# Even mixing part, sample group: an unread 128-column product of the identity among the narrow state products

## The chip, the cores and the metric

One core of a Trainium2 chip runs the whole kernel. The metric is the device time of one execution in microseconds; each version is executed several times and the median counts.

## What is computed

Two layers of a recurrent decoder are applied to a prompt of 2048 tokens and to a sample group of 8 sequences of 8 tokens each. The even layer runs retention heads and RWKV-7 heads side by side, the odd layer a gated delta rule. The sample sequences start from stored states, so each product of a query or a key with a state uses another state per sequence:

```python
# retention, per sequence b: queries times the state it starts from
o = jnp.einsum('bhck,bhkv->bhcv', qc * q_scale, S) + intra
# RWKV-7, per sequence b: keys and receptances read the state
s_kk = jnp.einsum('bhvk,bhk->bhv', S, kk_t)
S = S * exp(lw_t) - s_kk[..., None] * (kk_t * a_t)[:, :, None, :] + v_t[..., None] * k_t[:, :, None, :]
y = jnp.einsum('bhvk,bhk->bhv', S, r_t)
```

For the prompt one state serves all 128 tokens of a tile; for the samples each of the 8 states serves 8 tokens.

## The kernel before

The kernel runs four phases with a barrier after each: the even projection, the even mixing part (`mix_even_phase`), the odd projection, the odd mixing part. Tokens are worked in 17 tiles of 128: 16 of the prompt and, as tile number `PT`, the 64 sample tokens. The even mixing part is a software pipeline written out by hand. In a step, `t` is the tile whose right side, solve and outputs are made, `n` the tile ahead of it (scores, retention), `m` and `q` those ahead of that, and `p` the tile before, whose output projection (`project`, eight parts of six 512-column products) is laid between the others. Each engine has its own queue, in the order of the code, and they wait for each other by semaphores; what TensorE does is therefore exactly the order of the calls in the loop at the end of its block.

Two places of TensorE's queue handle the sample states:

- `ret_out(n)` with `n == PT` (line 1777 on): after the waits for the attention scores and for the loaded retention states it makes 32 products, each with a 64x128 stationary block (`sre`, a view of `me_xs`) and 8 moving columns of `qsT`, into banks `A_` and `B_`. VectorE copies them to `QST` (line 1350), and then the outputs of retention are made with the identity as moving operand, followed by `turn_mix(PT - 1)`, eight transposes.
- `sample_state_products(t)` with `t == PT` (line 1581 on), called first in `right_side(PT)`: 64 products, each with a 64x64 stationary block of `srw` (views of `me_th`, `me_kkr`, `me_ex2`) and 16 moving columns of `KR`, into bank `BX`; then `sample_ret_state(0, 0)`, VectorE's copy to `KST` (line 1344, in the trace `me_IL`), and `sample_ret_state(0, 1)`.

After these come, for tile `PT`, the products of `right_side` and `outputs_of_values` (a 128-column product of `KST` and the identity and two 64-column ones, eight times), `solve`, `project(PT - 1, 0)` and `outputs_of_solved`. All operands are plain f32 except those of `project`, which are rounded; a plain f32 product is two instructions (passes) in the trace, each with its own weight load. So the 32 products of the first place are 64 passes and the 64 of the second are 128 passes. A product's line in the trace is that of the helper `mm`, L1567; a transpose's is L1570.

Bank `BY` takes the results of `level_T`, which ScalarE copies out and counts in `s_ptc`; for tile `PT` there are two such levels (2 and 4). Later, `sample_ret_state` overwrites `BY`.

Of the kernel before, what the change touches and what calls it, by code (L numbers as in the profile page):

```python
# [12 lines left out]
P = 128  # L13
D = 1024
KD = D // P
SEQ, DEC_B, DEC_T = 2048, 8, 8
NS = DEC_B * DEC_T
PT = SEQ // P
# [562 lines left out]
def mix_even_phase(nc, t_in, out):  # L581
# [6 lines left out]
    with ctx:  # L588
# [3 lines left out]
        def sem(n):  # L592
            return new_semaphore(nc, sems, f"me_{n}")
# [16 lines left out]
        ident = ident_sb[:]  # L610
# [82 lines left out]
        A_, B_, C_, D_, BX, BY, BC = bk[3], bk[4], bk[2], bk[6], bk[7], bk[1], (bk[0], bk[5])  # L693
# [37 lines left out]
        s_ptc = sem("T_written")  # L731
# [19 lines left out]
        def levels_of(n):  # L751

            return [b for b in LEVELS[1:] if b < (DEC_T if n == PT else P)]

        LV = [sum(len(levels_of(i)) for i in range(n)) for n in range(NT + 1)]
# [6 lines left out]
        def await_(eng, name, n):  # L762


            if n >= 0:
                eng.wait_ge(E[name], n + 1)
# [798 lines left out]
        def _(pe):  # L1565
            def mm(o, l, r, start=True, stop=True):
                return nc.tensor.matmul(o, l, r, start=start, stop=stop)  # L1567

            def turn(o, i):
                return nc.tensor.transpose(o, i, ident)  # L1570

            def from_state(t, bank, b, which):


                o = bank[:, b * P:(b + 1) * P]
                if t == PT:
                    mm(o, KST[:, b, which, :], ident, start=b == 0, stop=False)
                else:
                    mm(o, KR[t % 2][:, b, which, :], s_wk[:, b].rearrange("p h v -> p (h v)"), start=b == 0, stop=False)

            def sample_state_products(t):
                pe.wait_ge(s_smp, 16 * 4)
                for b in range(4):
                    for q in range(DEC_B):
                        for p0 in (0, 64):
                            o = BX[p0:p0 + 64, b * P:(b + 1) * P].rearrange("p (w c) -> p w c", w=2)
                            last_op = mm(o[:, :, q * 8:q * 8 + 8], srw[b][p0:p0 + 64, q, :], KR[t % 2][p0:p0 + 64, b, :, q * 8:q * 8 + 8])
                last_op.then_inc(s_ks, 1)
                sample_ret_state(0, 0)
                pe.wait_ge(s_ksc, 1)  # L1590
                sample_ret_state(0, 1)

            def right_side(t):
                if t == PT:
                    sample_state_products(t)
                await_(pe, "o_copied", t)
                await_(pe, "state_new", t - 1)
                await_(pe, "mga_read", t)
                await_(pe, "mgb_read", t)
                for b in range(4):  # L1600
                    from_state(t, A_, b, 0)
                    for h in (2 * b, 2 * b + 1):
                        last_op = mm(A_[:, h * WN:(h + 1) * WN], MG[:, h, 0, :], tokV[t % 2][:, h, :], start=False, stop=h == H - 1)
                last_op.then_inc(E["rhs_ready"], 1)

            def outputs_of_values(t):
                await_(pe, "mixT_written0", t - 1)
                for b in range(4):
                    from_state(t, C_, b, 1)
                    for h in (2 * b, 2 * b + 1):  # L1610
                        mm(C_[:, h * WN:(h + 1) * WN], MG[:, h, 1, :], tokV[t % 2][:, h, :], start=False, stop=False)
# [162 lines left out]
            def ret_out(n):  # L1774
                v = tv[n % 2]
                pe.wait_ge(s_tv[n % 2], 16 * (n // 2 + 1))
                await_(pe, "att_written", n)
                await_(pe, "lengths_ready", min(n + 1, PT))
                await_(pe, "q_scaled", n)
                await_(pe, "ret_state_new", n - 1)  # L1780
                if n == PT:
                    for j in range(2):
                        pe.wait_ge(s_smr[j], 16)
                    for b in range(2):
                        for q in range(DEC_B):
                            for k, bank in enumerate((A_, B_)):
                                p0 = 64 * k
                                last_op = mm(bank[:, b * NS + q * 8:b * NS + q * 8 + 8], sre[b][p0:p0 + 64, q, :],
                                             qsT[p0:p0 + 64, b, q * 8:q * 8 + 8])
                    last_op.then_inc(s_qs, 1)  # L1790
                    pe.wait_ge(s_qsc, 1)
                for b in range(2):
                    if n < PT:
                        mm(A_[:, b * 256:(b + 1) * 256], qsT[:, b, :], s_ret[:, b].rearrange("p h v -> p (h v)"), stop=False)
                    for h in (2 * b, 2 * b + 1):
                        o = A_[:, h * RDV:(h + 1) * RDV]
                        if n == PT:
                            mm(o, QST[:, h, :], ident, stop=False)
                        last_op = mm(o, att[:, h, :], v[:, h * RDV:(h + 1) * RDV], start=False, stop=n == PT or h % 2 == 1)
                last_op.then_inc(E["ret_ready"], 1)  # L1800
# [55 lines left out]
            def sample_ret_state(b, r):  # L1856


                at = slice(r * Q, (r + 1) * Q)
                pe.wait_ge(s_mr, 2 * b + 2)  # L1860
                if b:
                    pe.wait_ge(s_mcr, 2)
                for half in range(2):
                    h, p0 = 2 * b + half, 64 * half
                    mm((BY, BX)[r][p0:p0 + 64, :], ks[at, h, :], vmr[h][at].rearrange("p q v -> p (q v)")).then_inc(s_mur, 1)
# [21 lines left out]
            for p, t, n, m, q in STEPS:  # L1887
# [74 lines left out]
                if n is not None:  # L1962
                    level_T(n, 64)
                    ret_out(n)
# [1219 lines left out]
```

## Time and profile before

| what | us |
|---|---|
| median of three executions (lowest, highest) | 3169.6 (3165.99, 3186.61) |
| the profiled execution | 3168.01 |
| its span, first to last instruction | 3166.2 |
| TensorE products, busy | 2978.1 (94% of the span) |
| VectorE, busy | 1864.6 (59%) |
| ScalarE, busy | 1032.0 (33%) |
| mean granted TensorE clock | 0.960 of full |

The busy shares are of the whole span; the granted clock is the share of 2.4 GHz that TensorE received, so that 1.00 is 2.4 GHz and 0.50 is 1.2 GHz. The profiled execution lies 1.6 us below the median. The even mixing part ends at about 1592 us of the span.

### The profile page before, as it was taken

The numbers are of one execution on the slowest core, as the hardware profiler recorded it, in microseconds if no ns is written. First come the engines' busy times: TensorE is split into PE (matmuls) and PEld (weight loads), VectorE is DVE, ScalarE is ACT, GpSimd is POOL, SyncE is SP. The second block draws the span as 40 slices with busy tenths as digits, with TensorE's granted clock in tenths as the row PEclk, the third lists the DMA queues.
The fourth block names the chain that finished last, engine by engine and source line by source line (L and its number), as shares of the span: only waits on it lengthen the run. The fifth ranks groups of instructions, "written<-read, shape, count | busy, mean of one in ns | idle before, by whom it ended". The sixth has DMA issues, their size and how long they took to land. (4 is left out here: it accounts for less than half of the span.)

```text
span 3166.2 us, 88698 instructions
## 1 busy us (share of the span) xinstructions
PE 2978.1 (94%) x38430; PEld 2714.3 (86%) x38430; DVE 1864.6 (59%) x3858; ACT 1032.0 (33%) x2337; POOL 502.9 (16%) x519
## 2 busy tenths in 40 slices
PE   8999999994899999999969999999995899999998
PEld 8999999993788888888769999999995788888886
DVE  4311222324677777777535156777665778887876
ACT  4211111113333443343157122222223344444441
POOL 0000000001333433333300000000001111111112
PEclk9999999996799999999889999999997899999998
DMA  5321212115233333343353221222114223333333
GB/s 166 99 73 60 73 64 69 67 49 170 71 97 115 120 111 118 112 126 122 100 176 110 75 69 61 74 75 70 66 47 158 72 82 96 95 96 95 94 98 127
DMA packets 222915, 302.15 MB, mean 95 GB/s; under 512 B 32184, under 2 KB 163520, under 8 KB 222528
## 3 DMA queue, kind: packets, MB, share of 16 engines
q1 hardware_dynamic: 213376, 266.54, 26.1%
q0 software_dynamic: 9152, 29.94, 3.0%
q8 instruction: 305, 5.00, 0.6%
q14 instruction: 82, 0.67, 0.1%
HBM read 200.70 MB, written 95.71 MB: 94 GB/s over the span
## 5 line engine op out<-in xcount | busy, mean ns | idle before, releaser
L363 DVE SCALAR_TENSOR_TENSOR po_stage<-po_work,po_cw,po_stage 128x424 f32<-128x424 f32 (+1 forms) x360 | 232.1, 645 | 27.6 <-issue 0.9
L476 PE MATMUL po_ps<-po_xnT_hi,po_w_hi 128*128 128x424 f32 x960 | 205.0, 355 | 0.0
L476 PE MATMUL po_ps<-po_xnT_hi,po_w_lo 128*128 128x424 f32 x960 | 204.4, 355 | 0.0
L476 PE MATMUL po_ps<-po_xnT_lo,po_w_hi 128*128 128x424 f32 x960 | 204.1, 354 | 0.0
L270 ACT ACTIVATE po_work<-po_ps 128x424 f32<-128x424 f32 (+1 forms) x120 | 61.6, 514 | 408.3 <-PE po_ps L476 408.3
L476 PEld LDWEIGHTS po_ps<-po_xnT_hi,po_w_hi 128*128 128x128 f32 x960 | 180.2, 188 | 5.2
L476 PEld LDWEIGHTS po_ps<-po_xnT_hi,po_w_lo 128*128 128x128 f32 x960 | 180.4, 188 | 4.5
L476 PEld LDWEIGHTS po_ps<-po_xnT_lo,po_w_hi 128*128 128x128 f32 x960 | 180.2, 188 | 4.6
L476 PE MATMUL pe_ps<-pe_w_hi,pe_xnT_hi 128*128 128x256 f32 x1088 | 154.9, 285 | 4.3 <-DVE pe_w_lo L382 3.6
L476 PE MATMUL pe_ps<-pe_w_lo,pe_xnT_hi 128*128 128x256 f32 x1088 | 153.4, 284 | 0.0
L476 PE MATMUL pe_ps<-pe_w_hi,pe_xnT_lo 128*128 128x256 f32 x1088 | 152.7, 283 | 0.0
L405 DVE TENSOR_SCALAR pe_stage<-pe_work,pe_cw 128x424 f32<-128x424 f32 (+1 forms) x65 | 28.2, 434 | 208.9 <-ACT pe_work L270 157.8
L476 PEld LDWEIGHTS pe_ps<-pe_w_hi,pe_xnT_hi 128*128 128x128 f32 x1088 | 140.8, 193 | 4.8 <-DVE pe_w_lo L382 4.0
L476 PEld LDWEIGHTS pe_ps<-pe_w_lo,pe_xnT_hi 128*128 128x128 f32 x1088 | 141.1, 193 | 0.0
L476 PEld LDWEIGHTS pe_ps<-pe_w_hi,pe_xnT_lo 128*128 128x128 f32 x1088 | 140.5, 192 | 0.0
L195 POOL DMA_DIRECT2D po_raw<-in_w_in_o x60 | 40.4, 677 | 622.4 <-DVE po_w_lo L382 621.8
L405 DVE TENSOR_SCALAR po_stage<-po_work,po_cw 128x424 f32<-128x424 f32 (+1 forms) x120 | 51.9, 433 | 143.8 <-ACT po_work L270 97.2
L195 POOL DMA_DIRECT2D pe_raw<-in_w_in_e x56 | 31.2, 557 | 581.1 <-DVE pe_w_lo L382 578.9
L1567 PE MATMUL me_b<-me_w_hi,me_mixT 128*128 128x512 f32 x272 | 120.8, 444 | 2.6 <-DMA me_ring<-scratch_w_lo 1.7
L270 ACT ACTIVATE pe_stage<-pe_ps 128x256 f32<-128x256 f32 x102 | 39.2, 384 | 254.5 <-PE pe_ps L476 254.4
L2823 PE MATMUL mo_b<-mo_w_hi,mo_mixT 128*128 128x512 f32 x272 | 120.1, 441 | 1.7 <-DVE mo_mixT_lo L2494 1.3
L363 DVE SCALAR_TENSOR_TENSOR pe_stage<-pe_stage,pe_ps 128x256 f32<-128x256 f32 x68 | 28.6, 421 | 157.4 <-ACT pe_stage L270 157.4
(453 smaller groups left out, 7169.3 us busy)
## 6 DMA issues: line engine op xcount, KB each, us to landing
me_ring<-scratch_w_lo SPq DMA_DIRECT2D x68, 512.0 KB, 3.8
mo_c<-scratch_ch_o SPq DMA_DIRECT2D x51, 512.0 KB, 3.5
scratch_ch_o<-po_stage SPq DMA_DIRECT2D x96, 212.0 KB, 1.9
scratch_tok_e<-pe_stage SPq DMA_DIRECT2D x136, 128.0 KB, 1.9
pe_raw<-in_w_in_e POOLq DMA_DIRECT2D x52, 256.0 KB, 3.7
me_xs<-scratch_ch_e SPq DMA_DIRECT2D x17, 768.0 KB, 6.2
po_raw<-in_w_in_o POOLq DMA_DIRECT2D x48, 256.0 KB, 3.8
scratch_ch_e<-pe_stage SPq DMA_DIRECT2D x52, 212.0 KB, 1.9
```

Source lines behind the costliest of these rows:

```text
L195: eng.dma_start(raw[r % RAW][:, :, 0:n], w_in[:, at:at + HK * n].rearrange("p (k n) -> p k n", k=HK)).then_inc(loaded(r)[0], 16)
L270: return nc.scalar.activation(o, i, f, **kw)
L363: return nc.vector.scalar_tensor_tensor(out=o, in0=a, scalar=s, in1=b, op0=op0, op1=op1)
L405: last = nc.vector.tensor_scalar(o, src, k, None, ALU.mult, ALU.bypass)
L476: last = nc.tensor.matmul(out, left.bitcast(F32R), right.bitcast(F32R), start=(i == 0 and k == 0), stop=(i == 2 and k == KD - 1))
L1567: return nc.tensor.matmul(o, l, r, start=start, stop=stop)
L2823: return nc.tensor.matmul(o, l, r, start=start, stop=stop)
```

## The change

A helper `keep_awake` issues a product of the identity with itself, 128 stationary columns and 128 moving ones, into the first 128 columns of `BY`, which nobody reads. In `sample_state_products` one is issued after every four narrow products (eight passes), but not after the last four: 15 in all. In `ret_out(PT)` one is issued in the middle of every four narrow products, 8 in all. There TensorE also waits first until ScalarE has copied all levels of tile `PT` out of `BY`.

```diff
+            def keep_awake(count):
+                for _ in range(count):
+                    mm(BY[:, 0:P], ident, ident)
...
             def sample_state_products(t):
...
                             last_op = mm(o[:, :, q * 8:q * 8 + 8], srw[b][p0:p0 + 64, q, :], KR[t % 2][p0:p0 + 64, b, :, q * 8:q * 8 + 8])
+                        if q % 2 and (b, q) != (3, DEC_B - 1):
+                            keep_awake(1)
...
                 if n == PT:
+                    pe.wait_ge(s_ptc, LV[PT + 1])
                     for j in range(2):
                         pe.wait_ge(s_smr[j], 16)
                     for b in range(2):
                         for q in range(DEC_B):
+                            if q % 2:
+                                keep_awake(1)
                             for k, bank in enumerate((A_, B_)):
```

## Rows read from the trace of the kernel before

**Rows 1.** The page, busy time and share of the span by engine

```profile
PE 2978.1 (94%) x38430; PEld 2714.3 (86%) x38430; DVE 1864.6 (59%) x3858; ACT 1032.0 (33%) x2337; POOL 502.9 (16%) x519
```

**Rows 2.** The page, 40 equal slices of the span: TensorE's granted clock in tenths

```profile
PEclk9999999996799999999889999999997899999998
```

**Rows 3.** Windows: stretch, length, busy by engine, granted clock, DMA share, GB/s

```profile
1520.34:1521.95 1.61, 1.61 (x30) 1.61 (x30) 1.53 (x2) 0.00 (x0) 1.30 (x2) 1.00 0.82 257
1521.95:1525.92 3.97, 3.97 (x39) 3.87 (x37) 1.24 (x2) 0.00 (x0) 2.57 (x3) 0.50 0.46 155
1526.50:1532.19 5.69, 5.69 (x30) 5.36 (x30) 0.00 (x0) 0.76 (x2) 5.69 (x10) 0.50 0.00 0
1532.19:1535.60 3.41, 3.41 (x122) 3.41 (x122) 2.37 (x4) 1.55 (x3) 3.24 (x3) 1.00 0.09 32
1535.60:1538.80 3.20, 3.20 (x21) 0.97 (x18) 0.69 (x1) 0.00 (x0) 2.52 (x2) 0.50 0.55 168
1538.80:1556.08 17.28, 17.28 (x77) 16.70 (x76) 1.38 (x2) 0.00 (x0) 0.00 (x0) 0.50 0.07 25
```

**Rows 4.** Timeline of TensorE (start, us, what): both narrow groups and what follows

```profile
1520.34 5.58 PE L1567 MATMUL me_b<-me_qsT,me_xs 64*128 64x8 f32 x64 [0.89 <-issue]
1526.50 0.80 PE L1567 MATMUL me_b<-me_ident,me_sq 128*128 128x128 f32 x2 [0.58 <-DVE me_sq L1350]
...
1530.08 1.91 PE L1570 MATMUL me_b<-me_ident,me_mix 128*128 128x128 f32 x8
1531.92 2.15 PE L1567 MATMUL me_b<-me_KR,me_th 64*64 64x16 f32 x64
...
1536.03 1.11 PE L1567 MATMUL me_b<-me_tokB,me_ks 32*64 32x512 f32 x1
```

**Rows 5.** Timeline of TensorE: tile PT's work behind the narrow groups

```profile
1540.13 0.74 PE L1567 MATMUL me_b<-me_ident,me_IL 128*128 128x128 f32 x2
1540.66 0.95 PE L1567 MATMUL me_b<-me_tokV,me_MG 128*128 128x64 f32 x4
...
1549.09 3.62 PE L1567 MATMUL me_b<-me_rhs,me_TF 128*128 128x64 f32 x16
1552.47 0.77 PE L1567 MATMUL me_b<-me_w_hi,me_mixT 128*128 128x512 f32 x1
...
1555.17 2.33 PE L1567 MATMUL me_b<-me_yw,me_G2T 128*128 128x64 f32 x16
1557.32 0.47 PE L1567 MATMUL me_b<-me_w_hi,me_mixT 128*128 128x512 f32 x1
```

**Rows 6.** Timeline of TensorE: the same kinds of work for the tile before

```profile
1487.66 1.06 PE L1570 MATMUL me_b<-me_ident,me_mix 128*128 128x128 f32 x8 [0.46 <-DVE me_IL L1207]
...
1489.18 0.44 PE L1567 MATMUL me_b<-me_s_wk,me_KR 128*128 128x128 f32 x2
1489.46 0.56 PE L1567 MATMUL me_b<-me_tokV,me_MG 128*128 128x64 f32 x4
1489.85 0.44 PE L1567 MATMUL me_b<-me_s_wk,me_KR 128*128 128x128 f32 x2
...
1495.82 1.97 PE L1567 MATMUL me_b<-me_rhs,me_TF 128*128 128x64 f32 x16
```

**Rows 7.** Windows: the stretch that rows 6 come from

```profile
1488.56:1497.72 9.16, 8.91 (x195) 8.58 (x193) 6.52 (x16) 2.10 (x4) 3.54 (x3) 1.00 0.26 85
```

**Rows 8.** Timelines of VectorE, GpSimd and ScalarE: what TensorE waits for there

```profile
1519.49 0.76 DVE L1207 TENSOR_TENSOR me_att<-me_b,me_tab_s 128x256 f32<-128x256 f32 x2 [0.85 <-PE me_b L1567]
...
1536.15 0.69 DVE L1344 COPY me_IL<-me_b 128x512 f32<-128x512 f32 x1 [1.07 <-PE me_b L1567]
...
1552.75 0.69 DVE L1207 TENSOR_TENSOR me_yw<-me_b,me_n 128x512 f32<-128x512 f32 x1 [7.84 <-PE me_b L1567]
...
1530.76 1.18 POOL L900 TENSOR_TENSOR me_qk<-me_tokV,me_seq 64x256 f32<-64x256 f32 x2
...
1504.66 0.38 ACT L1047 ACTIVATE me_TA<-me_b 128x256 f32<-128x256 f32 x1 [7.68 <-PE me_b L1567]
```

## The prediction

> **What bounds the kernel.** I read the page's busy shares first: TensorE's products take 94% of the span and no other engine is above 59% [rows 1], so wherever TensorE is neither idle nor kept waiting, its own time is the kernel's. The row of granted clocks came second: it is 0.9 or more nearly everywhere and dips at the joints of the phases [rows 2]; slices 20 and 21 (0.8 each) hold the end of the even mixing part, which is where the change lies. The third view, windows cut at the places where the clock changes, is the one that matters: there are two stretches at 0.50, that is 1.2 GHz. The first runs from 1521.95 to 1532.19 (10.2 us), the second from 1535.60 to 1556.08 (20.5 us); between them lie 3.4 us at 2.4 GHz [rows 3]. TensorE is busy in nearly all of it, so this is not time spent waiting. The timeline says what it did. The clock fell 1.6 us into the 8-column products of `ret_out`, after a pause of 0.89 us; it rose after some 5.7 us of 128-column products; it fell again at the end of 3.4 us of 16-column products. Then it stayed low through all of tile PT's right side, outputs and solve, which are 128- and 64-column products under 128-column weight loads [rows 3 to 5]. The same kinds of product one tile earlier ran at 1.00 throughout [rows 6, 7]. So this work keeps whichever clock it finds, and what was granted on entering it decides 17 us. Nobody but TensorE sets the pace here: VectorE, GpSimd and ScalarE are ahead of it except at the few places named below.
>
> **What a wide product costs.** One call is two passes of 128 columns. At 2.4 GHz such a pair, standing between narrower products, takes 0.28 us from its start to the next group's (1489.18 to 1489.46) [rows 6]; at 1.2 GHz it takes 0.53 (1540.13 to 1540.66) [rows 5]. The bounds: eight 128-column transposes end in 0.90 us, 0.11 a pass, so 0.22 a pair if nothing of the weight load shows; and 0.44, the whole record of a pair, if nothing overlaps; all [rows 6]. I take 0.28 and 0.53. All 23 at 2.4 GHz are 6.4 us (5.1 to 10.1).
>
> **The new wait.** ScalarE's last copy of a level of tile PT began at 1504.66 and took 0.38 [rows 8], 15 us before TensorE stands at that wait. It costs nothing, and not before 15 us of that cover were gone. Nothing reads what the wide products write; `BY` is next written by TensorE itself.
>
> **First place, `ret_out` (8 wide products).** Now 5.58 us [rows 4]: 30 passes at 2.4 GHz in 1.61 us, 0.054 each, and then 39 at 1.2 GHz in 3.97, 0.10 each (a window also counts the few that overlap its edges) [rows 3, 4]. If the clock holds: 64 x 0.054 = 3.5, plus 8 x 0.28 = 2.2, gives 5.7, a loss of 0.1. The retention outputs and transposes after it (1526.50 to 1531.92, 5.42 at 1.2 GHz [rows 4]) would take half, a gain of 2.7. If it falls as now, two wide products cost 0.28 and six 0.53, plus some passes that now slip into the slow part: a loss of 4.0, and the rise then comes somewhere within the 5.42 us that follow, a gain of 1.4 (0 to 2.7). The pause ahead of the place (0.89, until VectorE has the masked scores, 1519.49 + 0.76 [rows 8]) and the 0.58 behind it stay whatever is put between them.
>
> **Second place, `sample_state_products` (15 wide products).** Now 4.11 us, mostly at 2.4 GHz [rows 4]; 122 of the passes are in the 3.41 us at 2.4 GHz, 0.028 each, so all 128 at that clock are 3.6 [rows 3]. With 15 x 0.28 = 4.2 it is 7.8, a loss of 3.7 (2.8 to 6.1).
>
> **What follows, if the clock is kept.** `sample_ret_state` takes 2.77 us (1536.03 to 1538.80) [rows 3, 4]; at twice the clock it would be 1.4, but its second half waits for VectorE's copy (0.69 us, 1536.15), which can't start before the narrow products end [rows 8], so I take 2.0: a gain of 0.8. Right side and outputs, 1538.80 to 1549.09, 10.3 us, are eight equal groups; a group one tile earlier took 0.67 (1489.18 to 1489.85), eight make 5.4: gain 4.9. Solve: 3.38 against about 1.9, gain 1.5. The first part of `project`: 1552.47 to 1555.17, 2.70, half of it, 1.3. `outputs_of_solved` is at 1.2 GHz for its first 0.9 us, gain 0.3 [rows 3, 5, 6]. Together 8.0. The cover: VectorE's 0.69 us for the solved values starts at 1552.75 behind 2.7 us of `project` [rows 5, 8]; with `project` at 1.4 us it is still hidden, by 0.5. GpSimd has the values by sequence at 1531.94 [rows 8], and the state products that want them stand behind the parts of `project` that begin at 1557.32 [rows 5], still later when those begin 8 us earlier. What follows the outputs waits relative to them, so the whole tail, the barrier and the next phases move as they are.
>
> **The sums.** Both places hold: +0.1 - 2.7 + 3.7 - 0.8 - 8.0 = -7.7. First place falls, second holds: +4.0 - 1.4 + 3.7 - 0.8 - 8.0 = -2.5 (with the bounds of the price in both places and of the rise, -5.1 to +2.2).
>
> **Which one.** In the second place a wide product comes after 8 x 0.028 = 0.22 us of narrow passes, so wide work is over half of the time. In the first it comes after 8 x 0.054 = 0.43 us, 0.4 of the time, with a pause of 0.89 before it and one of 0.58 after. The clock there fell after only 1.6 us of narrow work, and by that point just two wide products would have been issued. I hold the first place for the weaker one and forecast that the clock still falls there and is kept in the second.
>
> The Trainium skill ("TensorE: Matmul & The Clock Gate", "Why this matters for your kernels") tells one to avoid idle gaps of TensorE between bursts of products, as what makes the clock drop. By that rule wide products among products that already run back to back change nothing, and only their price is left. The trace agrees for the first fall at most, which has a pause ahead of it; at the second TensorE was busy for 3.41 of 3.41 us.
>
> **The rivals.**
> - *Both hold*, 3168.0 - 7.7 = 3160.3 of the profiled execution. For it: eight-column passes load 64x128 blocks all the while, and 2.2 us of wide work is put among them. Against: the two pauses. Chance 0.30.
> - *Nothing is held* (the change doesn't do what it says: narrow passes or the pauses pull the clock down regardless, or VectorE's copy between the halves of `sample_ret_state` does). Its place is the entry into the right side at about 1538.8; its price +4.0 in the first place, and 12 x 0.28 + 3 x 0.53 = 5.0 in the second, less some 0.5 of rise: +8.5, 3176.5. It decides once the clock is at 1.2 GHz on entering the right side: then the 8.0 are gone, whatever the first place did. For it: `sample_ret_state`, eight passes on 32 rows with a wait inside, has no wide product, nor have the last eight narrow passes. Against: it is only about 2 us. Chance 0.15.
> - *First holds, second doesn't*: +0.1 - 2.7 + 3.7 = +1.1, 3169.1. Chance 0.08.
> - *First falls, second holds*: the forecast, chance 0.42. Other ways 0.05.
>
> **The numbers.** The sum gives 3168.0 - 2.5 = 3165.5 for an execution like the profiled one. That lies 1.6 below the median; where the clock changes relative to the work will differ from run to run, so I place the forecast between the two footings, 3166. Its own range is 3163 to 3172. Both hold reaches 3160.3, with a cheap wide product (0.22 instead of 0.28, 23 times, 1.4 us less) 3159; nothing held reaches 3176.5 and on the median's footing 3178. The three shown runs alone spread by 20 us. I give 3156 to 3178. All of it lies within 1% (31.7 us), about what a measurement of this kernel can tell from no change: same 0.95, faster 0.02, slower 0.03.
>
> **What would show it.** In the trace of the changed kernel: `ret_out`'s narrow group lasting 9 to 10 us with the clock at 0.50 before its end (5.7 at 1.00 if both hold); the second group about 7.8 us, at 1.00; the eight groups behind it 0.67 us apart and not 1.28, at 1.00; a pair of the identity 0.22 to 0.44 us of added time; the end of the even mixing part some 2.5 us earlier than 1592, and everything after it as before. The prediction is wrong if the eight groups are 1.28 us apart, if the first group shows 1.00 throughout, or if the odd part's length has moved by more than the even part's.

## The result

The changed kernel takes 3192.17 us (median of 14 executions, 3187.05 to 3204.45), the kernel before 3169.22 us in the 14 executions beside them. The ratio is 1.0071 (95% interval 1.0059 to 1.0083): 19 to 26 us slower, where 3166 was forecast with a range up to 3178. The change is smaller than the 1% that the prediction took for what a measurement can tell, but the interval lies wholly above 1.

The page of the changed kernel, busy shares and granted clock in 40 slices, to be read against [rows 1, 2]:

```profile
PE 2995.6 (94%) x38476; PEld 2727.2 (86%) x38476; DVE 1863.6 (58%) x3858; ACT 1031.7 (32%) x2337; POOL 503.0 (16%) x519
...
PEclk9999999996799999999689999999997899999999
```

TensorE is busy 17.5 us more, for 46 passes more; the other engines are where they were. Slice 20 went from 0.8 to 0.6: more time at 1.2 GHz and not less. The windows cut at the clock's changes, as in [rows 3]:

```profile
1528.65:1532.11 3.46, 3.46 (x36) 3.01 (x36) 2.78 (x3) 0.00 (x0) 1.76 (x3) 1.00 0.52 173
1532.11:1540.30 8.19, 7.60 (x47) 6.28 (x46) 0.49 (x2) 0.00 (x0) 8.19 (x13) 0.50 0.20 64
1540.30:1545.76 5.46, 5.46 (x26) 5.13 (x26) 0.00 (x0) 0.60 (x1) 5.04 (x5) 0.50 0.00 0
1545.76:1549.18 3.42, 3.42 (x50) 2.79 (x49) 2.37 (x4) 1.72 (x3) 0.94 (x1) 1.00 0.02 5
1549.18:1562.97 13.79, 13.79 (x110) 10.90 (x111) 0.00 (x0) 0.00 (x0) 0.00 (x0) 0.50 0.21 77
1562.97:1565.73 2.76, 2.76 (x10) 0.58 (x8) 0.69 (x1) 0.00 (x0) 0.00 (x0) 0.50 0.00 0
1565.73:1583.31 17.58, 17.58 (x79) 17.00 (x77) 1.38 (x2) 0.00 (x0) 0.00 (x0) 0.50 0.00 0
```

The first place begins at 1528.65, the second at 1545.72. In both the clock is at 1.00 for the first 3.4 us and then falls, in spite of the wide products, and on entering tile PT's right side (1565.73) it is at 0.50 as before. The timeline shows what a wide product costs, in the first place at 2.4 and at 1.2 GHz, then in the second likewise:

```profile
1529.94 0.49 PE L1567 MATMUL me_b<-me_ident 128*128 128x128 f32 x2
1530.36 0.61 PE L1567 MATMUL me_b<-me_qsT,me_xs 64*128 64x8 f32 x8
1530.90 0.49 PE L1567 MATMUL me_b<-me_ident 128*128 128x128 f32 x2
...
1535.02 0.79 PE L1567 MATMUL me_b<-me_ident 128*128 128x128 f32 x2
1535.75 1.03 PE L1567 MATMUL me_b<-me_qsT,me_xs 64*128 64x8 f32 x8
1536.70 0.79 PE L1567 MATMUL me_b<-me_ident 128*128 128x128 f32 x2
...
1546.06 0.49 PE L1567 MATMUL me_b<-me_ident 128*128 128x128 f32 x2
1546.48 0.41 PE L1567 MATMUL me_b<-me_KR,me_th 64*64 64x16 f32 x8
1546.82 0.49 PE L1567 MATMUL me_b<-me_ident 128*128 128x128 f32 x2
...
1554.10 0.79 PE L1567 MATMUL me_b<-me_ident 128*128 128x128 f32 x2
1554.83 0.61 PE L1567 MATMUL me_b<-me_KR,me_kkr 64*64 64x16 f32 x8
1555.37 0.79 PE L1567 MATMUL me_b<-me_ident 128*128 128x128 f32 x2
```

A turn of one wide product and eight narrow passes takes 0.96 us in the first place at 2.4 GHz (1529.94 to 1530.90); eight passes alone are 8 x 0.054 = 0.43, so the wide one adds 0.53. In the second place it is 0.76, less 8 x 0.028 = 0.22: 0.54. At 1.2 GHz the turns are 1.68 and 1.27 us; in the first place that is 1.68 - 8 x 0.10 = 0.88 for the wide one. The wide pair itself is followed by narrow work only after 0.42 us, and eight narrow passes behind it take 0.34 us in place of 0.22: time is lost on the way in and on the way out.

Summed by places: the narrow group of the first went from 5.58 to 11.05 us (1528.65 to 1539.70), the second from 4.11 to 17.25 (1545.72 to 1562.97): 5.5 + 13.1 = 18.6 us. What follows each of them is unchanged to 0.3 us. The two profiled executions differ by 23.0 us in span: 8.3 lie ahead of the first place, 18.6 from there to the outputs of tile `PT`, 0.8 from these to the end of the even mixing part (at 1619.8 us, and not at 1592.0), and the rest of the kernel is 4.8 shorter.

### The profile page after: what moved, and what is told of

Read it like the earlier page. It is cut to its first block and busy times, and to the rows that moved or that the text cites. A ratio compares the mean times of both kernels' runs of the same rounds, so it can differ in the third digit from the quotient of the medians.

```text
span 3189.2 us, 88791 instructions
## 1 busy us (share of the span) xinstructions
PE 2995.6 (94%) x38476; PEld 2727.2 (86%) x38476; DVE 1863.6 (58%) x3858; ACT 1031.7 (32%) x2337; POOL 503.0 (16%) x519
```

## The experiments

All times are medians; each ratio is to executions of the kernel before on the same chip, with its 95% interval, and 0.1% is 3.2 us. In kernels without the wide products of one or both places the arithmetic that counts is the same as in the kernel before, since nothing reads them.

**One place at a time.** Diffs against the changed kernel:

```diff
 # e1_ret_only: the second place's call is taken out
-                        if q % 2 and (b, q) != (3, DEC_B - 1):
-                            keep_awake(1)
 # e2_wk_only: the first place's call is taken out
-                            if q % 2:
-                                keep_awake(1)
```

> The eight wide products of the first place (the retention products) alone; none in the second. In the trace of the changed kernel the first narrow group with its wide products lasts 11.1 us against 5.6, and the clock falls in it as before. If each wide product simply costs what the trace shows there (about 0.52 us at 2.4 GHz, 0.82 us at 1.2 GHz, start to start, less the narrow passes) and nothing else has changed, the kernel is 5.5 us slower than before (about +0.17%). The rival: something outside the two places has changed with the kernel, since the trace of the changed kernel is already 8.3 us late when it reaches the first place; then the difference is 10 us or more.

Measured 3170.63 against 3167.35, ratio 1.0015 (1.0000 to 1.0029), 0 to 9 us slower. In its trace the first narrow group with the wait behind it lasts 11.5 us against 6.2. The rival of a change elsewhere is not needed for this one.

> The fifteen wide products of the second place alone; none in the first, so nothing stands between the narrow retention products. If the price is in the place itself: the second group lasts 17.3 us against 4.1 when the clock falls in its first third, so 13 us slower than before (+0.41%). If the fall of the clock depends on what the first place left behind, the group stays at 2.4 GHz (about 11.4 us) and the eight groups behind it too, which gives back 8.8: then within 2 us of before. The rival of a change elsewhere: 20 us or more slower.

Measured 3185.38, ratio 1.0061 (1.0045 to 1.0077), 14 to 24 us. So the two places' prices add up to the whole (0.15 + 0.61 against 0.71), and in its trace the second place behaves alike without the wide products of the first. Windows of the second place here:

```profile
1535.18:1538.37 3.19, 3.19 (x47) 2.59 (x46) 2.37 (x4) 1.72 (x3) 3.19 (x5) 1.00 0.02 5
1538.37:1552.39 14.02, 14.02 (x117) 11.13 (x116) 0.00 (x0) 0.00 (x0) 4.31 (x4) 0.50 0.23 76
1555.35:1571.73 16.38, 16.38 (x72) 15.80 (x71) 1.38 (x2) 0.00 (x0) 0.00 (x0) 0.50 0.00 0
```

Its clock, too, is lost 3.2 us after the group's start, and the place takes 17.4 us. The place accounts for 13 of the measured 14 to 24.

**More wide work.** Two products at each spot, in both places (e3), then in the second alone (e5):

```diff
-                keep_awake(1)
+                keep_awake(2)
```

> Two wide products in place of one at each of the 23 spots (46 in all). If wide work as such can hold the clock and there was too little of it: both places and the work behind them run at 1.00; a spot then costs 0.52 + 0.21 = 0.73 us, 16.8 in all, against 4.8 given back at the first place and its followers and 8.8 behind the second: about 3 us slower than before, so some 20 us faster than with one wide product. If unread products of the identity do not hold the clock at all: a spot costs 1.27 us at 1.2 GHz, and the kernel is 24 us or more slower than before.

Measured 3173.40, ratio 1.0020 (1.0006 to 1.0033), some 6 us slower than before, and thus some 16 us faster than with one wide product, though 23 more products are made. Windows from the start of the second place to the outputs of the solved values:

```profile
1533.08:1547.98 14.90, 14.90 (x189) 12.70 (x188) 2.37 (x4) 1.72 (x3) 2.03 (x2) 1.00 0.21 71
1547.98:1549.98 2.00, 2.00 (x16) 0.49 (x13) 0.69 (x1) 0.00 (x0) 0.00 (x0) 1.00 0.00 0
1549.98:1558.63 8.65, 8.65 (x72) 8.38 (x71) 1.39 (x2) 0.00 (x0) 0.00 (x0) 1.00 0.01 2
```

The clock is held, and the right side, outputs, solve and projection part take 8.65 us where they took 16.4: 7.7 us back, and 0.9 in the sample retention products. It does not pay, since the place itself costs 11 us more than before. In the first place the clock was held 7.9 us but lost before its end.

> Two wide products at each of the 15 spots of the second place, none in the first. If the clock is held by the amount of wide work among the narrow products of the place itself, the second group takes 14.9 us at 1.00 and the work behind it 8.65 + 2.0 as with two wide products in both places: +11.0 - 1.0 - 7.7, so 2 to 3 us slower than before. If what stands in the first place matters for the second, the clock falls in it and the kernel is 20 us or more slower.

Measured 3177.96, ratio 1.0038 (1.0024 to 1.0052), 8 to 16 us slower where 2 to 3 were expected. The profiled execution took 3188.85, the slowest but one of its twelve, and its windows of the place, of the sample retention products and of the work behind show what an execution can lose:

```profile
1535.85:1550.82 14.97, 14.97 (x189) 12.75 (x188) 2.37 (x4) 1.72 (x3) 7.62 (x8) 0.99 0.21 72
1550.82:1553.09 2.27, 2.27 (x18) 0.76 (x15) 0.69 (x1) 0.00 (x0) 0.00 (x0) 1.00 0.00 0
1553.09:1570.16 17.07, 17.07 (x77) 16.49 (x76) 1.38 (x2) 0.00 (x0) 0.00 (x0) 0.50 0.00 1
```

The place was held to its end, but behind the 2 us of sample retention products, which are on 32 rows and without wide work, the clock was lost 0.3 us into the right side, which then stayed at 0.50 for 17 us. The very same stretch, behind the same products, ran at 1.00 in the run before, so they are not shown to be the cause. Holding the clock through the narrow products is not sufficient, then: it can still be lost on entering the right side, and whether it is lost there was not the same in two executions that ran the same work from the second place on.

**A block ahead of the right side.** No wide product among the narrow ones, twelve in a row behind the sample retention products (the new wait ahead of the first place stays):

```diff
                 sample_ret_state(0, 1)
+                await_(pe, "h_ready", PT - 2)
+                for _ in range(12):
+                    mm(BC[1][:, 0:P], ident, ident)
```

> No wide product among the narrow ones; 12 of them in one block after the sample state products, just ahead of tile PT's right side (into a bank that the output projection overwrites). If the right side and what follows keep whichever clock they find, the block (5.1 us at 1.2 GHz, less once the clock is back) makes the clock rise within it, and the eight groups, the solve and the projection part run at 1.00: 8.65 us in place of 16.4. Cost about 4.4, gain 7.7: 3 us faster than before (-0.1%). If that stretch of work loses the clock by itself, the clock falls again in it and the kernel is 2 to 5 us slower than before.

Measured 3169.67, ratio 1.0010 (0.9995 to 1.0025), no difference that can be told. The mechanism is there: windows of most of the place, of what follows with most of the block, and of the right side to the projection part:

```profile
1538.56:1542.40 3.84, 3.84 (x127) 3.84 (x126) 2.37 (x4) 1.72 (x3) 3.84 (x5) 0.94 0.12 46
1542.40:1549.23 6.83, 6.83 (x35) 4.61 (x32) 0.69 (x1) 0.00 (x0) 3.89 (x4) 0.50 0.39 133
1550.02:1558.56 8.54, 8.54 (x72) 8.28 (x71) 1.38 (x2) 0.00 (x0) 0.00 (x0) 1.00 0.00 0
```

The right side keeps a clock that is high when it enters, for 8.5 us. The block cost 4.6 us for it (7.3 between the narrow group and the right side, where 2.8 stood), so 3 us should have been left, and the median does not show them. The trace does: from the start of the second place to the end of the even mixing part it takes 56.3 us, the two traces of the kernel before 60.1 and 61.8. The same execution took 794.5 us ahead of the first place, the most of all traces, so a gain of this size can drown in the scatter outside the places.

**The price of a wide product.** The unread product on half of the rows (e4, both places), with the narrow products' own 64x64 block (f1, second place), and all 15 in one block after half of the narrow products (f2, second place):

```diff
 # e4_half_rows
-                    mm(BY[:, 0:P], ident, ident)
+                    mm(BY[:, 0:P], ident[0:64, :], ident[0:64, :])
 # f1_same_block
-                            keep_awake(1)
+                            mm(BY[0:64, 0:P], ident[0:64, 0:64], ident[0:64, :])
 # f2_in_one, behind the loop over q, in place of the 15 calls
+                    if b == 1:
+                        keep_awake(15)
```

> The unread product reads rows 0 to 63 of the identity alone: a 64x128 stationary block and 128 moving columns, at the same 23 spots; all else as in the changed kernel. If its price comes from a 128x128 block that can't be loaded until the narrow products in both halves of the rows are done (and they not until it is), a half-row product lies beside the narrow ones of the other half and costs 0.21 to 0.3 us at 2.4 GHz, 0.43 to 0.6 at 1.2 GHz: the first group lasts 8 to 9.5 us and the second 9 to 13, the kernel 5 to 13 us slower than before. If the price is that of any change between kinds of product, the groups last as in the changed kernel, 11.1 and 17.3 us. The clock is not held in either case.

Measured 3183.52, ratio 1.0058 (1.0041 to 1.0075). The first place takes 7.5 us (8.1 with its wait), a little less than expected, the second 17.2, as with the full block. Timeline, first and second place:

```profile
1528.24 0.35 PE L1567 MATMUL me_b<-me_ident 64*128 64x128 f32 x1
1528.24 0.39 PE L1567 MATMUL me_b<-me_qsT,me_xs 64*128 64x8 f32 x2
...
1528.91 0.35 PE L1567 MATMUL me_b<-me_ident 64*128 64x128 f32 x1
...
1541.19 0.48 PE L1567 MATMUL me_b<-me_ident 64*128 64x128 f32 x2
1541.60 0.41 PE L1567 MATMUL me_b<-me_KR,me_th 64*64 64x16 f32 x8
1541.94 0.48 PE L1567 MATMUL me_b<-me_ident 64*128 64x128 f32 x2
```

In the first place, where the narrow blocks are 64x128 too, narrow passes start beside the unread product and a turn is 0.67 us, 0.24 for the unread one; in the second, where they are 64x64, the turn is 0.75, as with the full block. So reading half of the rows is not enough: in both places the unread block leaves the other half of the rows free, and it is cheap only where it has the shape of its neighbours.

> Second place only, at the same 15 spots, but the unread product has the narrow products' own block: 64x64 of the identity as stationary block, 128 moving columns. If the 0.52 us of a wide product there are the price of changing the shape of the block, to and from 64x64, this one costs what its two passes stream, about 0.21 us at 2.4 GHz and 0.43 at 1.2 GHz: a spot with its eight narrow passes takes 0.45 and 0.86 us, the place 8 to 11 us in place of 17, and the kernel is 4 to 7 us slower than before. If the price is that of 128 moving columns among short products whatever the block, the place takes 12 us at 2.4 GHz to 17 as with the full block. The clock is not held in either case.

```profile
1531.11 0.30 PE L1567 MATMUL me_b<-me_ident 64*64 64x128 f32 x1
1531.12 0.29 PE L1567 MATMUL me_b<-me_KR,me_th 64*64 64x16 f32 x2
1531.25 0.27 PE L1567 MATMUL me_b<-me_ident 64*64 64x128 f32 x1
1531.36 0.35 PE L1567 MATMUL me_b<-me_KR,me_th 64*64 64x16 f32 x6
1531.56 0.30 PE L1567 MATMUL me_b<-me_ident 64*64 64x128 f32 x1
```

A turn is 0.45 us, as expected: the same 128 moving columns, now at 0.23. The place took 7.8 us, the first 6.2 of them at 2.4 GHz; then the clock fell, and the right side ran at 1.2 GHz. Two passes of 128 columns in every 0.45 us, where e3 has four in every 0.98 and kept it, did not keep the clock to the end; what the full blocks of e3 have that these lack was not tested. Measured 3175.98 against 3165.80, ratio 1.0037 (1.0019 to 1.0055), which is 6 us or more, where the place explains 4.

> Second place only: the same 15 full wide products, but all in one block after half of the narrow ones, so that the shape of the block changes twice and not thirty times. If the change of shape is the price: 15 x 0.21 + 0.3 = 3.5 us at 2.4 GHz, the place about 7.3 us. As the last 64 narrow passes and the sample retention products after the block are 4 us without wide work, the clock is likely lost again on entering the right side: 3 to 4 us slower than before; if it is kept, 4 us faster. If each wide product costs 0.5 us wherever it stands: the place takes 11 us or more, and the kernel is 7 us slower.

```profile
1528.78 2.04 PE L1567 MATMUL me_b<-me_KR,me_th 64*64 64x16 f32 x64
1530.75 3.62 PE L1567 MATMUL me_b<-me_ident 128*128 128x128 f32 x30
1534.30 1.11 PE L1567 MATMUL me_b<-me_KR,me_kkr 64*64 64x16 f32 x32
```

The same 15 full products in one block take 3.55 us (1530.75 to 1534.30), 0.24 each, and the place 7.5 us (1528.78 to 1536.27). Measured 3169.66 against 3165.80, ratio 1.0021 (1.0005 to 1.0036): the clock was lost 0.6 us after entering the right side. The price is thus not the product's but that of changing the block's shape, twice a turn.

**Useful wide work.** In place of unread products, parts of the output projection of the tile before, which have to be made anyway:

```diff
 # x2_useful_second, against the kernel before, in sample_state_products
                 for b in range(4):
+                    if b == 2:
+                        project(PT - 1, 0)
...
                 sample_ret_state(0, 0)
+                project(PT - 1, 1)
                 pe.wait_ge(s_ksc, 1)
                 sample_ret_state(0, 1)
 # x3_three adds behind it
+                project(PT - 1, 2)
 # x12_useful_both: x2, and parts 5, 6, 7 of tile PT - 2 ahead of, amid and behind
 # the narrow products of ret_out
```

In the first of these the parts behind the moved ones each move up by two slots of the loop; in x3_three, and in x4_spread, which moves two parts like the first, they are spread so that parts 6 and 7 stay in their own slots:

```diff
 # x4_spread, against x2_useful_second; x3_three has (3, None, None, 4, 5, None, 6, 7)
             def slot(p, part):
                 if p == PT - 1:
-                    part += 2
+                    part = (2, 3, None, 4, 5, None, 6, 7)[part]
```

> No unread product at all: the first two parts of the output projection of the tile before (six 512-column products each, needed anyway) are moved into the second place, one between the second and the third block of narrow products, one between the two halves of the sample retention products; the later parts each move up by two slots. If wide work between the narrow products holds the clock, and useful work is free: second group about 5.2 us with its part, then the eight groups at 0.67 us and the solve at 1.00; from the start of the second place to the outputs of the solved values 17.3 us in place of 23.3, so 5 to 6 us faster than before, less what TensorE later waits where the moved parts used to lie (up to 2.8 us, but VectorE's chain sets the end there). If such moved work only opens waits elsewhere: within 1 us of before.

Measured 3163.70 against 3167.99, ratio 0.9994 (0.9979 to 1.0009). The mechanism held (right side to projection part 8.65 us at 1.00), but some of it was lost again at the end: TensorE waited 3.3 us for VectorE where the moved parts had lain, the last projection began at 0.50, and from the outputs of tile `PT` to the end of the even mixing part it took 39.7 us, against 36.9 and 38.3 in the two traces of the kernel before.

> As the run before, and in the first place too: the last three projection parts of tile PT - 2 stand in the pause ahead of the narrow retention products, between their two halves, and in the wait behind them. If it works in both places: the 0.89 us pause and the 0.58 us wait are filled, the narrow retention products run at 0.054 us a pass and what follows them at 1.00: another 5 to 6 us, 10 to 12 us faster than before (-0.35%). If the clock still falls around the first place, only the two waits (1.5 us) are gained on top of the run before.

Measured 3169.28, ratio 1.0007 (0.9993 to 1.0022): a miss. Timeline of the first half of the first place, of the part between the halves of the sample retention products, and of the right side:

```profile
1523.84 3.58 PE L1567 MATMUL me_b<-me_qsT,me_xs 64*128 64x8 f32 x32 [2.73 <-issue]
...
1543.85 0.49 PE L1567 MATMUL me_b<-me_w_hi,me_mixT 128*128 128x512 f32 x1
1544.14 0.63 PE L1567 MATMUL me_b<-me_w_lo,me_mixT 128*128 128x512 f32 x1
...
1547.03 0.79 PE L1567 MATMUL me_b<-me_ident,me_IL 128*128 128x128 f32 x2
...
1548.36 0.74 PE L1567 MATMUL me_b<-me_ident,me_IL 128*128 128x128 f32 x2
```

The pause ahead of the first place had been VectorE's time, not TensorE's: with parts 6 and 7 moved behind it, TensorE reached it earlier and waited 2.73 us in place of 0.89; the clock fell within that wait, at 1523.5. It came back in the first place, and the retention outputs ran at 1.00, but it fell again at 1543.9, in the middle of a projection part whose 512-column products follow without a gap, and the right side ran at 0.50 again, its first two groups 1.33 us apart. So this trace lost the 8 us behind the second place too, in spite of the projection parts there.

> Useful parts of the projection in the second place: part 0 after half of the narrow products, part 1 between the halves of the sample retention products, part 2 right ahead of tile PT's right side; the others spread over the later slots with the last two unmoved. If what decides is only that the clock is high on entering the right side, this is safer than two parts and gives the 8 us back in nearly every execution, for 1.4 us by which the outputs come later: 5 us faster than before (-0.15%). If late waits for VectorE eat it, as part of it was eaten with two parts moved (2.5 us at the output projection at the very end): 2 to 3 us faster.

Measured 3163.48 against 3172.47, ratio 0.9973 (0.9957 to 0.9989). Windows of the place with its three parts, and of the right side to the projection part:

```profile
1532.12:1542.89 10.77, 10.73 (x156) 7.61 (x156) 3.06 (x5) 1.72 (x3) 8.93 (x11) 1.00 0.29 100
1542.89:1551.42 8.53, 8.53 (x71) 8.27 (x70) 1.39 (x2) 0.00 (x0) 0.00 (x0) 1.00 0.21 61
```

The place (with the sample retention products) takes 10.8 us with three parts in it, 3.9 more than before, and 7.8 come back behind it; the last projection is as it was. This version beats both kernels, by 3.5 to 13.6 us against the kernel before.

> Parts 0 and 1 moved into the second place as in the run with two useful parts, but the later parts spread so that parts 6 and 7 stay where they were, ahead of VectorE's long chain. If the 2.5 us lost at the very end there came from the clock that fell in a wait of 3.3 us, they stay away: 5 to 6 us faster than before (-0.18%). If the second place sometimes loses the clock on entering the right side, as it did once, the median gains only 3 to 4 us.

Measured 3161.91, ratio 0.9978 (0.9960 to 0.9996). The profiled execution took 3174.80, well above that, and its windows say why:

```profile
1540.40:1544.23 3.83, 3.83 (x9) 1.30 (x8) 0.00 (x0) 0.00 (x0) 0.96 (x1) 0.50 0.29 111
1544.23:1560.62 16.39, 16.39 (x73) 15.81 (x72) 1.38 (x2) 0.00 (x0) 0.00 (x0) 0.50 0.00 0
```

The clock fell ahead of the right side, in spite of the two parts, and stayed low through it. So two parts do not hold it in every execution; the median gains nonetheless, and the interval (1 to 13 us) lies below the kernel before here too; it does not tell this version from the one with three parts. The traces speak for the clock, and not the new order of the parts, as what gains: from the start of the second place to the end of the even mixing part x3 takes 55.5 us and x2 57.6 with the clock kept, this one 65.7 without it, and the kernel before 60.1 and 61.8.

**The scatter.** The changed kernel and the kernel before, one trace more of each:

> The changed kernel once more, for a second trace. If the 8.3 us by which its first trace was late at the first place belong to the change, this trace is late again by 6 us or more against the kernel before (786.1 us from the start of the even mixing part to the first narrow product there, 794.3 in the changed one). If they are the scatter of the clock in the unchanged part, it may be anything from 783 to 795, as in the other traces so far. The two places themselves should again take 11.6 and 17 us, within 2 us.

> The kernel before once more, for a second trace. If the stretch ahead of the two places scatters by itself: another value than 786.1 us there, between 783 and 795; the two places again with the clock at 0.50 through the right side and the solve, 16.4 us.

From the start of the even mixing part to the first place the changed kernel now takes 786.6 us, where its first trace had 794.3; the kernel before takes 789.4, where it had 786.1. In the other traces of this study the stretch, whose code is the same in all but one of them, takes 783.3 to 794.5. So the 8.3 us of the first trace need no cause in the change; they lie within the scatter. From the start of the first place to the outputs of tile `PT` the changed kernel takes 18.2 us more than the kernel before in these second traces, 18.6 in the first ones. The clock did not fall at the same points, though: the second place took 15.7 us and not 17.3, since there it was at 1.00 for 5.8 us and not 3.4, and the first took 12.0. The right side ran at 0.50 again.

## Why the prediction was wrong

**The price of a wide product** was mis-sized, and this is the smaller of the two errors: 0.28 us with an upper bound of 0.44 at 2.4 GHz, 0.53 at 1.2 GHz. It is 0.53 and 0.88. Both rows it came from show a 128x128 pair among blocks of 128 rows, and the upper bound took for the worst that nothing overlaps within the pair. It left out the neighbours: between blocks of another shape the narrow passes stop overlapping as well, on either side. e4, f1 and f2 show this as the cause.

**The second place holds the clock**: this step failed, and it carried the result. "Wide work is over half of the time" divided 0.28 by 0.22 + 0.28. As measured, a turn is 0.76 us, and a pair that needs no change of shape adds 0.22 of it (0.98 - 0.76, the second pair in e3). The clock fell after 3.4 us, after 3.2 in e2 and after 5.8 in the second trace: in none of the three traces with one full wide product per turn did it reach the end of the place. With the clock gone the remaining turns cost 1.27 us each, and so the 3.7 us taken for this place became 13.1. That wide work among these products can hold the clock was right (e3, e5), though f1 leaves open what of it counts, and so was the order of the two places: with two wide products the second was held throughout and the first was not.

**What follows, if the clock is kept**: right. 8.0 + 0.8 us were taken; e3 gives 7.7 + 0.9. That this stretch keeps whichever clock it finds holds with one addition: it is at risk on entering, when the sample retention products lie just ahead (e5, f2).

**The first place falls as before**: right, at 5.5 us in place of 4.0, by the price. The rise within the retention outputs that was to give 1.4 us did not come in the first trace (5.42 us at 1.2 GHz, as before); in the second it did, and gave 0.8 us against the kernel before's second trace (4.43 and 5.21).

**Added up**: forecast was -2.5 us, and 18.6 were measured from the first place to the outputs. Of the 21.1 between them, the price in the first place is 1.5 and the rise that did not come 1.4. The second place is 9.4: 3.9 for the price alone (15 turns at 0.76 and the last narrow passes make 11.7 us, where 7.8 were taken), and 5.5 because most turns ran at 1.2 GHz. The other 8.8 are what was to come back behind it. With the clock kept and the true price the sum would have been about +3, within the range; the clock, 14 of the 21 us, took it out of it.

**The new wait** cost nothing: the pause ahead of the first place is 0.89 us in both kernels.

**The rivals**: "nothing is held" is what happened. It was given 0.15 and 3176.5, since twelve of its wide products were priced at 0.28 and the clock was left high through most of the second place. The sign that the prediction named for itself came up: the eight groups of the right side are 1.28 us apart (1567.07 to 1568.35). With the measured prices (four turns at 0.76, the rest at 1.27) it would have given 18.6 and 3186.6. The rule that the prediction cites from the Trainium skill ("TensorE: Matmul & The Clock Gate", "Why this matters for your kernels"), to avoid idle gaps between bursts of products, came out right in its result, not in its reason: TensorE was busy for 3.42 of 3.42 us ahead of the fall at 1549.18, so no idle gap stands ahead of it, and more wide work among the same products did keep the clock.

**What stays open**: the places explain 18.6 of the 23 us between the medians. e2 and f1, too, measured more than their place explains, 5 and 6.5 us by the medians, and x3 gained 9.0 where its second place and what follows it to the end of the even mixing part explain 4.6 to 6.3. The stretches outside the places scatter by 11 us from trace to trace (783.3 to 794.5 ahead of them), so this may be chance; it was not settled. Open is also why the clock falls where it does: most kernels have one trace, and the same work kept it in one and lost it in another (e3 and e5, x2 and x4).

## What to carry to other kernels

Look at the granted clock before anything is done about narrow products, and ask what work behind them inherits it: here 16 us of work at 1.2 GHz take 8.6 at 2.4. Products that are made only to keep the clock must be enough and cheap at once. Alternating them with blocks of another shape doubles their price; in one block, or in their neighbours' shape, they are cheap, but from within the narrow products neither of these kept the clock through the right side (f2, f1). A block right ahead of the right side did, for 4.6 us of cost against 7.8, without a gain that the median shows (e6). The only versions measured faster than the kernel before use wide work that has to be done anyway, moved to the spot (x3, x4); what it covered before must be able to do without it, as the waits in x2 and x12 show.

## What the runs showed of the hardware

- With 128 moving columns at 2.4 GHz, a 128x128 f32 product costs 0.24 us among its like (f2) and 0.53 us between 64x64 or 64x128 blocks (the changed kernel); a 64x128 one 0.24 between 64x128 blocks and 0.53 between 64x64 ones (e4); a 64x64 one 0.23 between 64x64 ones (f1).
- TensorE busy without a gap lost its clock: 3.42 of 3.42 us ahead of 1549.18, with a pair of 128-column passes in every 0.76 us; with two pairs in every 0.98 us it kept it for 14.9 us (e3). With two 128-column passes under 64x64 blocks in every 0.45 us it lost it after 6.2 us (f1), and in x12 it lost it amid 512-column products under 128x128 blocks.
- The same 16 us of 128- and 64-column products ran at 1.2 GHz throughout when entered so, and in 8.5 to 8.65 us at 2.4 GHz in four of the six traces that entered it high (e3, e6, x2, x3); in the other two (e5, f2) the clock fell 0.3 and 0.6 us after the entry.
